# Expert chunks that finish their own output rows, with two weight buffers and permuted normalised rows

## What is computed

```python
def rms_norm(x, g):
    y = xf * lax.rsqrt(jnp.mean(xf * xf, axis=-1, keepdims=True) + EPS)
    return (y * g).astype(x.dtype)

def expert_ffn(xb, wg, wu, wd):
    return (jax.nn.silu(xb @ wg) * (xb @ wu)) @ wd

# encoder_layer
h = rms_norm(x, lp['norm1_g'])
z = h @ lp['w_in']                      # 1024 -> 2048: u, v, x_b, g_b
...                                     # two mixers
x = x + jnp.concatenate([out_a, out_b], axis=-1) @ lp['w_out']
h2 = rms_norm(x, lp['norm2_g'])
moe = hier_moe(h2, ...)                 # top-1 of 4 groups, top-2 of 8 experts; y = sum of gate * expert_ffn
x = x + moe
...                                     # after the layer: y = rms_norm(x, final_norm_g)
```

## Time and profile before

| | us |
|---|---|
| median of 3 executions | 1779.95 (1779.68 to 1780.24) |
| the profiled execution | 1778.52 |
| its span, first to last instruction | 1776.9 |
| PE busy in the span | 1670.4 (94%) |
| DVE, ACT, POOL busy | 602.5, 365.5, 345.5 |

### The profile page before, as it was taken

The page is one execution under the profiler, slowest core; times in us unless marked ns, Lnnn a source line. Parts: engine busy times, 40 slices in busy tenths (PEclk is TensorE's granted clock), DMA queues, the critical chain, the costliest instruction groups (busy, mean ns, idle before and its releaser), DMA issues.

```text
span 1776.9 us, 28305 instructions
## 1 busy us (share of the span) xinstructions
PE 1670.4 (94%) x10574; PEld 1424.8 (80%) x10574; DVE 602.5 (34%) x1770; ACT 365.5 (21%) x768; POOL 345.5 (19%) x536
## 2 busy tenths in 40 slices
PE   7999999999999999997599999999999999999950
PEld 4768676767676676764599999999999999999950
DVE  3536363545464554644211111111111111111114
ACT  2314131413132231322011111111111111111113
POOL 1001111111111010101112222222222222222225
PEclk9999999999999999998699999999999999999985
DMA  9410202011010101026288999899999999999968
GB/s 307 177 72 2 83 12 83 12 60 35 36 59 36 59 12 71 1 60 173 81 251 236 278 279 280 254 291 290 300 303 304 314 319 310 321 323 327 314 184 347
DMA packets 221004, 322.25 MB, mean 181 GB/s; under 512 B 24889, under 2 KB 173274, under 8 KB 220970
## 3 DMA queue, kind: packets, MB, share of 16 engines
q1 hardware_dynamic: 200538, 264.07, 44.8%
q0 software_dynamic: 17984, 48.81, 12.9%
q10 hardware_dynamic: 2448, 8.91, 1.2%
HBM read 268.97 MB, written 52.78 MB: 181 GB/s over the span
## 4 chain that ended last, share of the span: by engine, by line
PE 93%; DMA 2%; DVE 2%; POOL 1%; issue 1%; ACT 1%; SPq 0%; ACTq 0%; POOLq 0%; DVEq 0%
PE ps L838 28%; PE ps L700 19%; PE ps L851 14%; PE ps L761 13%; PE ps L723 7%; PE ps L860 3%; PE ps L822 2%; PE ps L783 2%; PE ps L733 2%; PE ps L687 1%; PE ps L775 1%; PE ps L746 1%; DMA w_in_sb<-acc_rows 1%; DMA out_y<-w_in_sb 0%; POOL rstd L666 0%
## 5 line engine op out<-in xcount | busy, mean ns | idle before, releaser
L838 PE MATMUL ps<-w_out_sb,w_in_sb 128*128 128x128 f32 (+4 forms) x4096 | 509.5, 285 | 1.3 <-ACT w_out_sb L977 1.3
L838 PEld LDWEIGHTS ps<-w_out_sb,w_in_sb 128*128 128x128 f32 x4096 | 506.0, 190 | 1.6 <-issue 1.6
L700 PE MATMUL ps<-hT,w_in_sb 128*128 128x256 f32 (+1 forms) x1728 | 360.5, 369 | 3.0 <-issue 3.0
L700 PEld LDWEIGHTS ps<-hT,w_in_sb 128*128 128x128 f32 x1728 | 313.6, 191 | 46.2 <-issue 7.2
L851 PE MATMUL ps<-w_out_sb,w_in_sb 128*128 128x128 f32 (+4 forms) x2048 | 259.0, 287 | 0.0
L851 PEld LDWEIGHTS ps<-w_out_sb,w_in_sb 128*128 128x128 f32 x2048 | 252.5, 190 | 0.2
L761 PE MATMUL ps<-w_out_sb,catT 128*128 128x512 f32 x544 | 237.1, 596 | 5.5 <-DVE catT L1171 5.5
L337 POOL TENSOR_TENSOR pad<-mhalf 128x1 f32<-128x1 f32 x149 | 34.0, 228 | 1041.1 <-ACT h2T L886 240.0
L761 PEld LDWEIGHTS ps<-w_out_sb,catT 128*128 128x128 f32 x544 | 103.4, 192 | 132.8 <-issue 127.0
L1324 DVE TENSOR_TENSOR w_out_sb<-ps,w_out_sb 128x128 f32<-128x128 f32 (+4 forms) x128 | 39.3, 307 | 469.5 <-ACT w_out_sb L983 469.5
L1328 DVE COPY w_out_sb<-ps 128x256 f32<-128x256 f32 (+4 forms) x128 | 58.3, 456 | 224.0 <-PE ps L851 224.0
(11 more groups left out here) (185 smaller groups left out, 1244.6 us busy)
## 6 DMA issues: line engine op xcount, KB each, us to landing
w_in_sb<-in_w_gate SPq DMA_DIRECT2D x64, 1024.0 KB, 7.1
w_in_sb<-in_w_up SPq DMA_DIRECT2D x64, 1024.0 KB, 9.5
w_in_sb<-in_w_down SPq DMA_DIRECT2D x32, 1536.0 KB, 9.6
w_in_sb<-in_w_down SPq DMA_DIRECT2D x32, 512.0 KB, 9.4
xa<-in_x SPq DMA_DIRECT2D x17, 512.0 KB, 4.0
xr<-in_x SPq DMA_DIRECT2D x17, 512.0 KB, 3.3
acc_rows<-xr SPq DMA_DIRECT2D x17, 512.0 KB, 2.6
w_in_sb<-acc_rows SPq DMA_DIRECT2D x17, 512.0 KB, 7.7
```

The lines of the kernel that those rows point to most:

```text
L700: mm = pe.matmul(bank[:, cc * n:(cc + 1) * n], w_in_v[:, k, col:col + P], hT[:, k, 0:n], start=(k == 0), stop=(k == KD - 1))
L838: mm = pe.matmul(bank[:, m * CH:m * CH + size], w[:, k, f * P:(f + 1) * P], xTm[:, k, :, 0:size // 2], start=(k == 0), stop=(k == KD - 1))
```

## The change

The final pass is gone. Each chunk now gathers the rows of `acc_rows` that it adds to (`part`, from POOL), DVE evicts all four banks with `part` added, ACT squares the sum, POOL makes the root, and DVE writes the normalised rows `yfin`. POOL writes the sum back to `acc_rows` and `yfin` to `y`, both by indirect writes. A row is visited by two chunks; the second one's write stands. Indirect transfers carry a bounds check that leaves out slots with no row, so the zero rows at the end of `acc_rows` and `h2_rows` and their four stores are gone.

The expert weights have two whole buffers: the second lies in the upper quarter of `w_in_sb` and in mixer tiles that are free by then. Chunks are therefore worked in pairs, and each loop's end is rounded up to an even number of chunks from the beginning; at least two chunks fall to each size. Gate and up are loaded whole, 4096 numbers in a run for each partition (rows `(p k)` instead of `(k p)`). To match, DVE writes the normalised mixer rows with their columns permuted (`by_k`), into `catT`'s memory, no longer in place. DVE's write of `catT` then waits for the store of these rows.

```diff
+        rows_m = sb("rows_sb", [P, 2, GT, D])
+        xa, xr = rows_m[:, 0], rows_m[:, 1]
+        cols_m = sb("cols_sb", [P, 2, KD, G])
+        hT, catT = cols_m[:, 0], cols_m[:, 1]
+        h2 = catT.rearrange("p k n -> p (k n)").rearrange("p (t d) -> p t d", t=GT)
...
+        o = KD * DE
+        wg_e = [x.rearrange("p (k f) -> p k f", k=KD) for x in (w_in[:, 0:o], w_in[:, 3 * o:4 * o])]
...
@@ sync
-            sp.wait_ge(const_dve, 3)
-            for dst in (acc, h2_rows):
-                for h in range(2):
-                    r = NTOK + HF * h
-                    sp.dma_start(dst[r:r + HF], zrow[0:HF]).then_inc(table_ready, 16)
...
-                for piece, job in enumerate(("gu1", "gu3", "y2", "y3")):
-
-                    wait_full(sp, "chunk", q - 1, job)
-                    weights(e, piece)
...
+            e = expert(1)
+            gate_up(e, 1)
+            down(e, 1)
+            with sp.Fori(2, chunks, 2) as q:
+                for i in range(2):
+                    e = expert(q + i)
+                    wait_full(sp, "chunk", q + i - 2, f"gu{KE - 1}")
+                    gate_up(e, i)
+                    wait_full(sp, "chunk", q + i - 2, f"y{KD // 2 - 1}")
+                    down(e, i)
@@ gpsimd, the loop over the chunks
-                load_index(q, idx_out, io_loaded)
+                pool.wait_ge(nx_loaded, 16 * q + 16)
+                carried(5 * q + 1)
+                nc.gpsimd.tensor_copy(idx_out[:], idx_nx[:]).then_inc(io_ready, 1)
+                pool.wait_ge(io_ready, q + 1)
+                carried(5 * q + 2)
+                for h in range(2):
+                    pool.indirect_dma_start(part[:, h, :], None, acc,
+                                            bass.IndirectOffsetOnAxis(ap=idx_out[:, h, 0:1], axis=0),
+                                            bounds_check=NTOK - 1, oob_is_err=False).then_inc(part_loaded, 16)
+                load_index(q + 1, idx_nx, nx_loaded)
                 pool.wait_ge(xg_loaded, 32 * q + 64)
                 load_index(q + 2, idx_in, ix_loaded)
                 pool.wait_ge(ix_loaded, 16 * q + 48)
                 wait_full(pool, "chunk", q, "xT3")
...
                 gather()
...
+                carried(5 * q + 4)
                 for h in range(2):
                     pool.indirect_dma_start(acc, bass.IndirectOffsetOnAxis(ap=idx_out[:, h, 0:1], axis=0),
-                                            ysb[:, h, :], None, compute_op=ALU.add).then_inc(y_added, 16)
-
-                pool.wait_ge(y_added, 32 * q + 32)
+                                            ysb[:, h, :], None,
+                                            bounds_check=NTOK - 1, oob_is_err=False).then_inc(part_stored, 16)
+                pool.wait_ge(y_stored, 32 * q + 32)
+                pool.wait_ge(ysq_ready, 2 * q + 3)
+                carried(5 * q + 5)
+                nc.gpsimd.tensor_copy(idx_y[:], idx_out[:]).then_inc(iy_ready, 1)
+                nc.gpsimd.tensor_scalar(rstd[0:HF, 0:2], ssq[0:HF, 0:2], 1.0 / D, EPS, ALU.mult, ALU.add)
+                pool.wait_ge(yms_ready, q + 1)
+                nc.gpsimd.tensor_tensor(rstd[0:HF, 0:2], rstd[0:HF, 0:2], mhalf[0:HF, 0:2], ALU.pow)
+                pool.wait_ge(iy_ready, q + 1)
+                pool.wait_ge(yfin_ready, 2 * q + 2)
+                carried(5 * q + 6)
+                for h in range(2):
+                    pool.indirect_dma_start(a["y"], bass.IndirectOffsetOnAxis(ap=idx_y[:, h, 0:1], axis=0),
+                                            yfin[:, h, :], None, ...).then_inc(y_stored, 16)
+                pool.wait_ge(part_stored, 32 * q + 32)
@@ tensor
-                        mm = pe.transpose(bank[:, k * P:(k + 1) * P], rows[:, t, kk * P:(kk + 1) * P], ident[:])
+                        mm = pe.transpose(bank[:, k * P:(k + 1) * P], h2[:, t, kk * P:(kk + 1) * P], ident[:])
...
-                with pe.Fori(ends[k], ends[k + 1]) as q:
-                    chunk(q, size)
+                with pe.Fori(ends[k], ends[k + 1], 2) as q:
+                    for i in range(2):
+                        chunk(q + i, i, size)
@@ scalar, a chunk
+                for h in range(2):
...
+                    nc.scalar.activation(junk[0:size // 2], ysb[0:size // 2, h], ACT.Square,
+                                         accum_out=ssq[0:size // 2, h:h + 1]).then_inc(ysq_ready, 1)
@@ vector
+                for t in range(prev):
+                    dve.wait_ge(h2_stored[t], 16 * g)
...
-                    if seg != "last":
-                        dve.wait_ge(acc_stored[t], 16 * g + 16)
-                    V.scalar_tensor_tensor(out=(xa if seg == "last" else xr)[:, t], in0=xr[:, t], ...)
+                    V.scalar_tensor_tensor(out=by_k(h2[:, t], 0), in0=by_k(xr[:, t], 1), scalar=rstd[:, GT + t:GT + t + 1],
+                                           in1=by_k(g2b[:], 1), op0=ALU.mult, op1=ALU.mult).then_inc(h2_ready[t], 1)
...
+            plink(V.tensor_scalar(pairs[:], cend[:, :, NE], 0.5, 0.25, ALU.mult, ALU.add))
...             (some ten small instructions that round the loop ends to even numbers)
@@ vector, a chunk
+                dve.wait_ge(io_ready, q + 1)
+                dve.wait_ge(part_loaded, 32 * q + 32)
                 for i in range(2):
+                    for h in range(2):
+                        bank = wait_full(dve, "chunk", q, f"r{i}{h}")
+                        V.scalar_tensor_tensor(out=ysb[...], in0=bank[0:size // 2, :], scalar=idx_out[...],
+                                               in1=part[...], op0=ALU.mult, op1=ALU.add)
+                dve.wait_ge(yrs_ready, q + 2)
+                dve.wait_ge(y_stored, 32 * q + 32)
+                for h in range(2):
+                    V.scalar_tensor_tensor(out=yfin[0:size // 2, h], in0=ysb[0:size // 2, h], scalar=rstd[0:size // 2, h:h + 1],
+                                           in1=g1b[0:size // 2], op0=ALU.mult, op1=ALU.mult).then_inc(yfin_ready, 1)
```

More of the change, by code:

```diff
@@ L507, in _ @@
-            for b in range(FB):
-                load_f(0, b)
-            with sp.Fori(1, NTILE // FB) as it:
-                for b in range(FB):
-                    load_f(it, b)
-            load_f(NTILE // FB, 0)
+            sp.wait_ge(acc_stored[0], 16 * (NPG + 1))
+            sp.wait_ge(h2_stored[0], 16 * (NPG + 1))
+            wait_out(sp, "plan", 0, "plan")
+            chunks = sp.value_load(plan[0:1, 2 * P + len(SIZES) - 1:2 * P + len(SIZES)], min_val=2 * len(SIZES), max_val=P - 2)
@@ L518, in _ @@
                 sp.wait_ge(h2_stored[t], 16 * n)
-            for b in range(FB):
-                sp.wait_ge(f_stored[b], 16 * (NTILE // FB + (b == 0)))
         @block.gpsimd
@@ L671, in _ @@
-            with pool.Fori(0, NTILE // FB) as it:
-                for b in range(FB):
-                    final(it, b)
-            final(NTILE // FB, 0)
+                                            ysb[:, h, :], None,
[4 more added lines that the diff above has]
+                nc.gpsimd.tensor_copy(idx_y[:], idx_out[:]).then_inc(iy_ready, 1)
@@ L984, in chunk @@
                 x_columns("chunk", q, size)
-                act.wait_ge(io_loaded, 16 * q + 16)
-                for i in range(2):
-                    bank = wait_full(act, "chunk", q, f"r{i}0")
-                    nc.scalar.activation(ysb[0:size // 2, 0, i * BANK:(i + 1) * BANK], bank[0:size // 2, :], ACT.Copy,
-                                         scale=idx_out[0:size // 2, 0, 1:2].bitcast(F32)).then_inc(read("chunk", f"r{i}0"), 1)
+                for h in range(2):
+                    for i in range(2):
+                        wait_out(act, "chunk", q, f"r{i}{h}")
+                    act.wait_ge(ysq_ready, 2 * q + 1 + h)
+                    act.wait_ge(yrs_ready, q + 1)
+                    nc.scalar.activation(junk[0:size // 2], ysb[0:size // 2, h], ACT.Square,
+                                         accum_out=ssq[0:size // 2, h:h + 1]).then_inc(ysq_ready, 1)
+            act.nop().then_inc(ysq_ready, 1)
             x_columns("pre", 0, CH)
@@ L1338, in _ @@
                     chunk(q, size)
-            dve.wait_ge(fg_loaded, 16)
-            def final(it, b):
-                dve.wait_ge(f_rs, it * FB + b + 1)
-                V.scalar_tensor_tensor(out=fb[b], in0=fb[b], scalar=rstd[:, b:b + 1], in1=g1b[:],
-                                       op0=ALU.mult, op1=ALU.mult).then_inc(f_ready, 1)
-            with dve.Fori(0, NTILE // FB) as it:
-                for b in range(FB):
-                    final(it, b)
-            final(NTILE // FB, 0)
 def kernel(**inputs):
```

228 lines of the change are left out of this document (99 added, 129 removed).

## The result

| | before | after |
|---|---|---|
| median | 1779.82 us | 1857.55 us |
| ratio | | 1.043 [1.0416, 1.0444] |
| profiled execution | 1778.52 us | 1861.37 us |
| its span | 1776.9 us | 1859.8 us |
| chunk stage (first gate and up products to PE's stop) | 848.2 us | 968.4 us |

The changed kernel is 4.3% slower; forecast were 1766 us and a range up to 1810. (The median of before is that of the runs beside the changed kernel.) One of the four executions of the changed kernel took 2997.79 us at a granted clock of 0.555 and is left out of the ratio; the other three took 1852.62, 1853.73 and 1861.37. The end did become short. The stage ahead of it grew by three times as much.

The account below looks back on a forecast made before the run. PE bounds the kernel before; after, POOL's 26.0 us loop exceeds the smaller chunks. Span 1776.9 - 45 + 6.7 + 0.6 = 1739; adding 3.05 to the median, 1742; plus 24 delay, 1766 us. Range 1741 to 1810.

Parts of the forecast that it names:

- The end: From PE's stop to the program's end, with the final pass removed: 17 us instead of 62.3, saving 45 us.
- The pairs: Rounding loop ends to even chunk counts adds no chunk but enlarges three: 6.7 us more PE work.
- the plan: Ten small added instructions make the plan 2 us later, hidden by PE's 3.92 us wait for gathered rows.
- the permuted rows: Strided normalising of mixer rows: hidden at group boundaries except in the last group, 0 to 1.3 us, taken as 0.6.
- the weights on PE: Expert weight loads, fewer and larger, two buffers ahead: no effect on PE.
- Steps 1 to 6 and 8: POOL's loop: sum write 3.35, root 1.8, `yfin` 2.6, `y` write 3.35, `part` gathers 4.1, index loads 2.7, next-row gather 3.1 us.
- step 5: In POOL's loop, index copy, two carries and two gathers of `part`: 4.1 us, the sum's landing already over.
- the second rival: Row writes with bounds check cost 1.53 us each: loop 28.2 us, delay 68, time 1810; chance 0.22.
- step 7: POOL's wait for the second index load, queued behind the gathers of `part`: 5.0 us, between 3.4 and 6.5.
- the sentence after step 8: Eviction is over by the loop's end: `part` landing plus four evictions 11.4 us, against 11.8 for rest of steps 5 to 8.
- the third rival: Row transfers held up by 16-KB weight runs: step 7 grows by 3.8, loop 29.8 us, delay 111, time 1853; chance 0.08.
- The delay: POOL's loop of 26.0 us outlasts the smaller chunks: 24 us added at the end, PE standing still some 20.

Follow-up runs that it names:

- e3: The changed kernel without the weight loads of chunks 2 to 31, its two buffers filled once and reused; 1746.33 us in one run.
- e9: The changed kernel with the slot numbers of the next gather loaded one step earlier, before `y`'s write, 16-KB weight runs kept; 1846.09 us, 1.0396.
- e4: The changed kernel with the bound of the `y` write set to skip every slot but row 0; 1829.58 us in one run.

## Why the prediction was wrong

**What held.** The pairs, the plan, the permuted rows, the weights on PE: together they give PE's stop at 1722 without weights, measured 1722.0, with two errors that cancel (e3). The loop ends are 4, 12, 18, 24, 32. Steps 1 to 6 and 8: in the loop shown above they take 27.8 - 9.6 = 18.1 us, where I had 21.0; on the mean loop 30.5 - 9.7 = 20.8, with the wait of step 5 in it. Plain writes of rows took 0.94 to 1.05 (medians 0.96 and 0.99), so the second rival, at 1.53, fell. Half of PE's idle time is where I put it, ahead of the down products (38.8 us, for DVE's multiply); the other half, 37.4, is ahead of the next chunk's transposes, which I hadn't named. In the last group the strided normalising took 2.05 us:
```profile
835.65 2.05 DVE L1170 SCALAR_TENSOR_TENSOR cols_sb<-rows_sb,rstd,g2b 128x1024 f32<-128x1024 f32 x1 [2.40 <-POOL rstd L541]
```
against 1.27 in the earlier trace rows, 0.8 more, between the 0.6 taken and the upper end of 1.3. The Trainium skill's rule on 16-byte lines, cited ahead of the result (SBUF — State Buffer, DMA port swizzle), pointed the right way; the upper end that I set beside it was not reached.

**The step that failed is the landing of the partial sums' gather, in step 7 and in the sentence after step 8.** Step 7 had 5.0 us, between 3.4 and 6.5, and measured 9.7. I took it from a landing of 8.2 us beside 1- and 3-KB runs, of which 3.7 had gone, and left the kernel's new 16-KB runs to the third rival: a loop of 29.8 us, a delay of 111, 1853 us, at a chance of 0.08. Measured were a loop of 30.5, 115 us of the profiled execution against the run without weights, and 1853.7. One of the signs that I had put down for being wrong came with it: PE stood still in the 156-row chunks, from 1105 us on. The mechanism and nearly its size were written down; its chance was wrong, and the range, which left it out, with it. The reason that I should have weighed is in the diff: the runs of gate and up grew by 16, and 4 MB of them go out at once, while the row of 8.2 shows that runs of 1 and 3 KB already double the quiet 4.4.

**The sentence after step 8 weighed more.** "By then the eviction is over" set the partial sums' landing against the other steps, 11.4 against 11.8 us. Both rest on the same landing, so both grew, and which of the two waits ended last is in the chain that ended last, here from 1300 to 1800 us:
```profile
by line: DMA gate_sb<-acc_rows,idx_out 34.6%; issue 19.1%; DMA acc_rows<-w_out_sb,idx_out 18.5%; DVE w_out_sb L1326 6.4%; POOL acc_rows L655 3.1%; DVE gate_sb L1333 2.7%; DMA idx_in<-slot_table 2.6%; POOL pad L339 2.5%; POOL out_y L671 2.3%
```
It goes by the partial sums, 34.6%, and hardly by the slot numbers, 2.6%; that is why e9 gained so little. In the prediction's own terms this path was there to be priced: steps 1 to 5 up to the second gather, 14.2, and then 11.4 for landing and eviction are 25.6 us, as long as the sum of 26.0 and with no slot number in it. Likewise step 5, costed at no wait, took 45.7 us over 10 loops; the landing of the sums has 18.5% of that chain.

**The delay.** I counted a late loop as PE standing still. Of the 115 us, 39.5 are PE busy for longer, at a mean granted clock of 0.95 instead of 1.00. After a stall of 2.17 us a chunk's 64 down products took 9.13 us; a chunk later, after 1.59, 63 of them took 7.35:
```profile
1529.98 9.13 PE L851 MATMUL ps<-w_out_sb,cols_sb 128*128 128x132 f32 x64 [2.17 <-DVE w_out_sb L1316]
...
1557.86 7.35 PE L851 MATMUL ps<-w_out_sb,w_in_sb 128*128 128x132 f32 x63 [1.59 <-DVE w_out_sb L1316]
```
From 1530 to 1535 the granted clock was 0.66, between TensorE's two levels (1.00 is 2.4 GHz, 0.50 is 1.2 GHz). The length of the one stall doesn't decide it: after 2.34 us, at 1436, the clock stayed at the upper level, and after 1.31 us, at 1744, it was 0.81:
```profile
1530.00:1535.00 5.00, 5.00 (x29) 5.00 (x30) 0.43 (x1) 0.00 (x0) 3.57 (x6) 0.66 1.00 429
1436.00:1443.50 7.50, 7.50 (x66) 7.50 (x67) 1.30 (x4) 0.00 (x0) 5.72 (x9) 1.00 1.02 408
1744.00:1753.20 9.20, 9.11 (x67) 9.12 (x68) 1.31 (x4) 0.00 (x0) 5.79 (x9) 0.81 0.98 409
```
PE's time was not what set the pace there, as the chain above lists no line of PE, so these 39.5 us are not a second loss beside the idle ones: a shorter loop takes both away, as e3 shows.

**The end** was 22.8 us and not 17. The last write of `y` is issued at 1848.12, 11.1 us after PE's stop, where the sum had 12.2, and takes 0.95; its landing has a median of 3.7 us there, and then the trace shows nothing for some 8 us up to 1859.8. The run without weights has the same gap; before, the last store of `y` (issued at 1771.31, 3.6 to land) left some 2 us. So the gap is the term that the sum lacked. What fills it wasn't tried and stays open.

Against the sum: it put the span at 1739 + 24 = 1763, and 1859.8 was measured, 96.8 more. The end gives 22.8 - 17 = 5.8 of that, and the loop 115 - 24 = 91.

**Where the cover was.** Before, POOL's loop held one landing of rows: the accumulating write, for which it waited 138.4 us over 17 chunks between 1300 and 1714 (8.1 each, put down to the index load behind it), and then the slot numbers, 76.8 over 17 (4.5). It still had time left, 41.0 us of waiting for DVE's evictions, since PE set the pace:
```profile
POOL idx_out L609 <- issue: 138.4, 17, 9.3
POOL pad L337 <- DMA idx_in<-slot_table: 76.8, 17, 6.1
POOL pad L337 <- DVE w_in_sb L1332: 41.0, 15, 5.5
```
The change put a second landing of rows, an addition and a second write into that loop, and set its gather and its slot numbers behind 4 MB of longer runs.

## What to carry to other kernels

When a change turns an accumulating write into gather, add and write, price the loop as a chain of landings first, and take their length beside the traffic that the change itself makes. Merging loads into longer runs took less of the engines here (a share of 0.95 at 330 GB/s with 4-KB runs, 1.00 at 310 with 1-KB runs), but the row transfers behind a burst of 16-KB runs landed later (the gather of sums in 9.8 us against 7.3 with 1-KB runs), while the write of sums landed sooner (4.6 against 8.8). With the short chain 4-KB runs did better than 1-KB ones; 16-KB runs were not tried with it. Where two waits of nearly equal length lie side by side, removing one shows little; ask the chain which of them ends last.

## What the runs showed of the hardware

- From 900 to 1700 us row gathers of the sums land at the median in 4.4 us alone, 7.3 beside 1-KB weight runs, 9.0 beside 4-KB runs and 9.8 beside 16-KB runs issued 4 MB at a time; in the moment of such a burst the engines were at a share of 1.00 and 429 GB/s. The median doesn't order the times: 4-KB runs (1798.8 us) lie near 1-KB runs (1794.9) and far from 16-KB runs (1853.7).
- A plain indirect write of 4-KB rows holds POOL for 0.94 to 1.05 us, about as one of small entries; the accumulating one of the same rows took 1.48 to 1.54. With a bounds check the gather of `h2_rows` took 1.04 us at the median, without one 0.98.
- Leaving out nearly all rows of `y` by the bound took 17.8 MB off POOL's queue but none of its 32416 packets (e4).
- A DVE pass over 128 x 1024 elements whose two inputs are read with a stride of eight elements took 2.05 us, and 1.27 in order.
- A stall of 2.17 us on PE was followed by 5 us at a granted clock of 0.66, one of 1.31 by 9.2 us at 0.81, and ones of 1.59 and 2.34 by 1.00.
